# The low halves of the weights move from the Vector engine to GpSimd, and the gated delta rule starts on its queries and keys

## The chip, the cores and the metric

The kernel runs on 1 core of one Trainium2 chip. The metric is the device time of one execution in microseconds (us). Three runs of the kernel before gave 2921.94, 2924.85 and 2926.3 us; the median is 2924.85 us.

The engines are called by their profile names: PE is TensorE (PEld is its weight load), DVE is VectorE, ACT is ScalarE, POOL is GpSimd, SP is SyncE, which here only issues weight transfers.

## The reference

Everything is float32, for 256 tokens of width 2048. Two layers of the first kind each normalize x, multiply by a matrix with 6,668 columns (`w_in`) and feed three mixers: a sliding-window attention (12 query heads, 4 key heads), a convolution module with 31 taps over 512 channels, and a gated delta rule with 6 heads of 128. Their outputs are gated, joined and multiplied by `w_out`.

```
h = rms_norm(x, norm_w[l]);  p = h @ w_in[l]
oa = sliding_window_sink_attention(qa, ka, va, sinks[l]) * silu(za)
ob = conformer_conv_module(ub, ...) * silu(zb)
oc = rms_norm(gated_deltanet(qkv_c, b_c, a_c, ...)) * silu(zc)
x = x + concat([oa, ob, oc]) @ w_out[l]
# inside gated_deltanet:
qkv = silu(causal_depthwise_conv(qkv_raw, conv_w))   # 4 taps, 2304 channels: q, k, v of 768 each
q = l2_norm(q);  k = l2_norm(k)
# then, in chunks of 64 tokens: decays, (I + lower)^-1, a scan over four chunks
```

Two more layers follow, one with a pooling mixer (trailing means over 2, 4, 8 and 16 tokens, then a matrix per group) and one with a gated linear recurrence (LRU: a 4-tap convolution, two block-diagonal gate matrices, a scan over the tokens). Each has its input and output matrices of width 4096 and a gated per-layer embedding after it ("post").

## The kernel before, in words

**Weights.** All matrices lie in one long array (`wall`) in the order in which they are used, cut into chunks, most of them 128 partitions x 2048 floats (1 MB). `sync` (L367) loads chunk c into `W[c % 3]`. For most matrices (`SPLIT`, 388 chunks) the product is made of three passes in the float32r type: ACT copies the chunk into `WH` (the high part, `high`, L857), DVE computes `WL = W - WH` (the low part, `low`, L1340), the activations are split likewise into `HH`/`HL`, `YH`/`YL` or `DH`/`DL`, and PE adds low x high, high x low and high x high (L412). `W`, `WH` and `WL` have three buffers each. The load of chunk c waits for the low part of chunk c-3; the high part of chunk c waits until PE is done with the third chunk before it. The gate matrices of the LRU and two small matrices are used unsplit from `W`; the load behind such a chunk waits for PE itself.

**One program for each engine.** The five functions `tensor`, `vector`, `scalar`, `sync` and `gpsimd` are written out in order, and an engine issues strictly in its order. `tensor`, `vector` and `scalar` walk through the same list of chunks. PE works on a `Group` of chunks (four for 512 columns), whose results lie in a pair of PSUM banks; ACT or DVE take them out behind `group(n)`, which waits for the last chunk. In `tick()` ACT first issues the high part of the chunk two ahead, and DVE the low part of the chunk two ahead, then both call `pump()` four times; PE calls `pump()` four times in a chunk too.

**Side work.** `pump()` moves each active generator one `yield` on. The generators are the delta rule (`decays`, `delta_net`), the convolution (`conformer`, DVE only for its 124 taps), the 4-tap filter of the delta rule (`taps`), `attention`, and in the LRU `conv` and `chain`. The same generator exists for several engines and its `yield` and `rest(n)` counts are set by hand so that the same step comes at the same pump on each. `finish(g)` runs the rest of a generator at once. A generator's step that waits holds up all that the engine's program has behind it, the next high or low part included.

**Around the change.** In `block1` the six groups behind the first eight chunks are the group with 268 columns and the four that give the delta rule its inputs (i = 4, 0, 1, 2, 3 in ACT's and DVE's code; i = 0 to 2 hold queries, keys, 768 channels each, i = 3 and 4 the values). Before, both engines finish the filter and the decays after i = 3 and then begin `delta_net`. In the LRU, `chain(n)` is begun after gate chunk n and has three steps with one `yield` between them, so that all three fall into one tick. `gpsimd` issues only transfers: x to memory and back around each block (its place is scratch meanwhile), a small input and two gain rows for each post stage.

Of the kernel before, what the change touches and what calls it, by code (L numbers as in the profile page):

```python
# [5 lines left out]
F32 = mybir.dt.float32  # L6
# [198 lines left out]
def rest(n):  # L205

    for _ in range(n):
        yield
# [25 lines left out]
def program(nc, wall, tab, pos_d, pT_d, xin, gpost_d, gplo_d, xsave, out):  # L234
# [6 lines left out]
    with ctx:  # L241
# [135 lines left out]
        def gpsimd(e, w):  # L377
            xs_d = xsave.rearrange("(t p) c -> p t c", t=2)
            for l in range(2):
                if l == 0:  # L380
                    for g in range(4):
                        w.wait_ge(*to(f"x{g}", 0))
                else:
                    w.wait_ge(*to("ev_v", 19))
                e.dma_start(xs_d, X[:, :, :]).then_inc(*up("saved", l, by=16))
                w.wait_ge(*to("saved", l))
                w.wait_ge(*to("at_p", l, "turn", 8))
                e.dma_start(X[:, :, :], xs_d).then_inc(*up("back", l, by=16))

            def load_pt(l):  # L390
                e.dma_start(Q[:, 21760:22272], pT_d[:, 512 * l:512 * l + 512]).then_inc(*up("pT", l, by=16))

            def pre_post(l):
                e.dma_start(GP, gpost_d[l:l + 1, :].to_broadcast([128, 2048])).then_inc(*up("gpost", l, by=16))
                e.dma_start(GL, gplo_d[l:l + 1, :].to_broadcast([128, 2048])).then_inc(*up("gple", l, by=16))

            w.wait_ge(*to("norm_v", 2, "hl", 15))
            load_pt(0)
            w.wait_ge(*to("y_v", "pool", 3, 1))
            pre_post(0)  # L400
            w.wait_ge(*to("chunk", ple_end))
            load_pt(1)
            w.wait_ge(*to("y_v", "lru", 7, 1))
            pre_post(1)

        def tensor(e, w):
# [110 lines left out]
            def delta_net(l):  # L517
                yield from rest(3)
# [30 lines left out]
                yield  # L549
                for src, which in ((CV, "tv"), (CK, "tk")):  # L550
                    for k in range(3):
                        b = side(("dn", l, which, k), ("dn_v", l, which, k))
                        for j in range(4):
                            us = slice(128 * (4 * k + j), 128 * (4 * k + j) + 128)
                            i = e.transpose(b[:, 128 * j:128 * j + 128], src[:, us], ident)
                        i.then_inc(*up("dn_p", l, which, k))
                    yield from rest(2)
# [88 lines left out]
            def attention(l):  # L646
# [4 lines left out]
                yield from rest(12)  # L651
# [31 lines left out]
                yield from rest(3)  # L683
                scores(1)
                yield from rest(4)
# [3 lines left out]
                yield from rest(4)  # L689
                turned(1)  # L690
                yield from rest(4)
                turned(2)
                yield from rest(2)
# [17 lines left out]
            def block1(l):  # L711
                proj(l, 512)
                proj(l, 512)
                cf = begin(conformer(l))
                proj(l, 256, "cm+")
                dc = begin(decays(l), first=True)
                for _ in range(4):
                    proj(l, 512)
                finish(dc)
                dn = begin(delta_net(l), first=True)  # L720
                proj(l, 512)
                proj(l, 256)
# [111 lines left out]
        def scalar(e, w):  # L834
# [87 lines left out]
            def delta_net(l):  # L922
                act(sc(0, 3072), sc(4662, 3072), ACT.Square, "dn_a", l, "sq")
# [52 lines left out]
            def attention(l):  # L976
# [8 lines left out]
                yield from rest(12)  # L985
# [24 lines left out]
                yield from rest(3)  # L1010
                scores(1)
                yield from rest(4)
# [3 lines left out]
                yield from rest(4)  # L1016
                turned(1)
                yield from rest(4)
                turned(2)
                yield from rest(2)  # L1020
                yield

            def block1(l):
                w.wait_ge(*to("norm_v", l, "hl", 15))
# [80 lines left out]

            def pool_layer():
# [21 lines left out]
                mix_end = {}  # L1128
                load_u(0)
                for g in range(4):  # L1130
                    for i in range(2):
                        gi = group(4)
                        if g:
                            w.wait_ge(*to("y_v", "pool", g - 1, 1))
                        for b in range(2):
                            act(ZT[:, 4 * i + 2 * b:4 * i + 2 * b + 2, :], pair(bank(gi, b)), ACT.Silu,
                                *(("ev_a", gi) if b else ()))
                    if g > 0:
                        out_part(0, g - 1)
                        oend = here["c"] - 1  # L1140
                    finish(here["win"])
                    for i in range(2):
                        gi = group(2)
                        w.wait_ge(*to("ev_v", gi))
                        if g:
                            w.wait_ge(*to("chunk", oend))
                        act(YH[:, 4 * i:4 * i + 4, :], ZT[:, 4 * i:4 * i + 4, :], ACT.Copy, "y_a", "pool", g, i)
                    mix_end[g] = here["c"] - 1
                    if g < 3:
                        load_u(g + 1)  # L1150
                out_part(0, 3)

            def lru_layer():
# [13 lines left out]
                def chain(n, gi):  # L1167
# [9 lines left out]
                    yield  # L1177
# [3 lines left out]
                    yield  # L1181
# [46 lines left out]
                finish(ch)  # L1228
                out_part(1, 3, halves=2)

            def post(l, n):
                rstd(3 + 4 * l, SM[:, 12:14])
                for i in range(4):
# [9 lines left out]
                    for t in range(2):  # L1243
                        act(E[:, t, 512 * i:512 * i + 512], bank(gi, t), ACT.Copy, *(("ev_a", gi) if t else ()))
                for i in range(4):
                    sumsq(4 + 4 * l, i, JUNK, X, ("x_v", "mid", l, i))
# [41 lines left out]
        def vector(e, w):  # L1288
# [45 lines left out]
            def low(c):  # L1334

                if c >= NCH or c not in split_no:
                    return
                s, m = split_no[c], chunks[c][3] * chunks[c][5]
                w.wait_ge(*to("hi", c))
                e.tensor_tensor(WL[:, s % NSPL, 0:m], W[:, c % NRAW, 0:m], WH[:, s % NSPL, 0:m].bitcast(F32),  # L1340
                                ALU.subtract).then_inc(*up("lo", c))
# [111 lines left out]
            def delta_net(l, zc):  # L1453
                yield from rest(3)
# [108 lines left out]
            def attention(l):  # L1563
# [27 lines left out]
                yield from rest(4)  # L1591
# [36 lines left out]
                yield from rest(3)  # L1628
                scores(1)
                weights(0)  # L1630
                yield from rest(4)
                scores(2)
                weights(1)
                yield from rest(2)
                turned(0)
                weights(2)
                yield from rest(4)
                turned(1)
                yield from rest(4)
                turned(2)  # L1640
                yield from rest(2)
# [7 lines left out]
            def block1(l):  # L1649
# [8 lines left out]
                w.wait_ge(*to("saved", l))  # L1658
                zero(RAW[:, :, 0:3])
                for i in (4, 0, 1, 2, 3):  # L1660
# [7 lines left out]
                    tp = begin(taps(l, i, 4 if i < 4 else 2, g))  # L1668
                finish(tp)
                finish(dc)  # L1670
                dn = begin(delta_net(l, g + 2), first=True)
# [111 lines left out]
            def lru_layer():  # L1783
# [19 lines left out]
                def chain(n, gi, zg):  # L1803
# [12 lines left out]
                    yield  # L1816
# [4 lines left out]
                    yield  # L1821
# [76 lines left out]
            low(0)  # L1898
            low(1)
# [82 lines left out]
```

## Time and profile before

| | |
|---|---|
| runs, us | 2921.94, 2924.85, 2926.3 |
| profiled execution, its own time | 2930.08 us |
| its span | 2928.3 us |
| granted TensorE clock, mean | 0.938 of full |
| PE busy | 2615.5 us (89%) |
| DVE busy | 1683.6 us (57%) |
| ACT busy | 1220.8 us (42%) |
| POOL busy | 6.4 us |
| DMA | 430.61 MB, 147 GB/s |

The profile shows one execution. A row of the views gives a line of the kernel, an engine, an operation, the tensors (out<-in) with their shapes, and how often. Engines overlap, so that busy times don't add to the span; what matters is when PE is idle and who ended its wait. Many rows carry L1305, L1309, L1314 or L843: those are the helpers `tt`, `stt`, `ts` of DVE and `act` of ACT, so that one goes by the tensors there. `Q` is the big scratch, `SM` small columns, `TB` the table of constants, `PS` is PSUM.

### The profile page before, as it was taken

How to read it: one execution, taken by the hardware profiler on the slowest of the kernel's cores; microseconds unless marked ns; L12 is line 12 of the kernel's file. 1: busy time of each engine (PE TensorE's matmuls, PEld its weight loads, DVE VectorE, ACT ScalarE, POOL GpSimd, SP SyncE). 2: the span in 40 equal slices, each digit the busy share in tenths (PEclk: the TensorE clock that was granted, in tenths of full speed). 3: DMA queues.
4: the chain of work that ended last, by engine and by line, in shares of the span. 5: the costliest groups of instructions: out<-in, count | busy, mean ns of one | idle time of the engine just before them, and what ended most of it. 6: DMA issues, size and time to landing. Idle time of an engine off the chain costs nothing.

```text
span 2928.3 us, 39683 instructions
## 1 busy us (share of the span) xinstructions
PE 2615.5 (89%) x17372; PEld 2405.0 (82%) x17372; DVE 1683.6 (57%) x1866; ACT 1220.8 (42%) x1273; POOL 6.4 (0%) x14
## 2 busy tenths in 40 slices
PE   7987998699969996999999999989888988879788
PEld 7986978579969876789989999867888877778666
DVE  4687745555868545555645556655655456445654
ACT  4433234443432244344444334354544444444453
POOL 0000000000000000000000000000000000000000
PEclk9998989899989998999999999999899998989899
DMA  6441222354422212545455545535333434334433
GB/s 223 146 159 73 102 72 103 115 215 146 144 104 98 87 64 109 180 160 184 171 202 187 187 173 188 221 128 200 116 139 145 176 130 172 145 138 164 158 129 129
DMA packets 62493, 430.61 MB, mean 147 GB/s; under 512 B 6896, under 2 KB 7024, under 8 KB 12272
## 3 DMA queue, kind: packets, MB, share of 16 engines
q1 hardware_dynamic: 60496, 414.97, 38.8%
q0 software_dynamic: 1824, 13.11, 1.1%
q8 instruction: 136, 2.23, 0.3%
q14 instruction: 37, 0.30, 0.0%
HBM read 421.76 MB, written 6.29 MB: 146 GB/s over the span
## 4 chain that ended last, share of the span: by engine, by line
PE 69%; DVE 17%; ACT 8%; issue 4%; DMA 2%; DVEq 0%; SPq 0%; ACTq 0%
PE PS L412 68%; DVE WL L1340 4%; ACT Q L843 4%; DVE Q L1309 3%; ACT WH L857 3%; DVE Q L1305 3%; DVE Y L1309 2%; DMA W<-in_wall 2%; DVE Q L1829 1%; DVE X L1309 1%; DVE Q L1314 1%; ACT L843 0%; DVE SM L1324 0%; DVE Q L1316 0%; PE PS L660 0%
## 5 line engine op out<-in xcount | busy, mean ns | idle before, releaser
L1340 DVE TENSOR_TENSOR WL<-W,WH 128x2048 fp32r<-128x2048 f32 (+2 forms) x388 | 860.7, 2225 | 858.8 <-ACT WH L857 858.7
L857 ACT ACTIVATE WH<-W 128x2048 fp32r<-128x2048 f32 (+2 forms) x388 | 717.9, 1858 | 738.9 <-PE PS L412 706.1
L412 PE MATMUL PS<-HH,WL 128*128 128x256 f32 x3392 | 577.4, 291 | 110.7 <-DVE WL L1340 110.0
L412 PEld LDWEIGHTS PS<-HH,WL 128*128 128x128 f32 x3392 | 484.9, 197 | 119.6 <-DVE WL L1340 113.4
L412 PE MATMUL PS<-HL,WH 128*128 128x256 f32 x3392 | 566.7, 288 | 0.0
L412 PE MATMUL PS<-HH,WH 128*128 128x256 f32 x3392 | 564.3, 287 | 0.0
L412 PEld LDWEIGHTS PS<-HL,WH 128*128 128x128 f32 x3392 | 483.2, 197 | 0.0
L412 PEld LDWEIGHTS PS<-HH,WH 128*128 128x128 f32 x3392 | 480.7, 196 | 0.0
L412 PE MATMUL PS<-WL,HH 128*128 128x512 f32 (+2 forms) x768 | 232.3, 384 | 21.8 <-DVE HL L1305 21.8
L412 PE MATMUL PS<-WH,HL 128*128 128x512 f32 (+2 forms) x768 | 225.3, 374 | 0.0
L412 PE MATMUL PS<-WH,HH 128*128 128x512 f32 (+2 forms) x768 | 223.8, 372 | 0.0
L843 ACT ACTIVATE Q<-PS 128x512 f32<-128x512 f32 (+1 forms) x136 | 80.5, 592 | 297.5 <-PE PS L412 268.6
L412 PE MATMUL PS<-Q 128*128 128x128 f32 (+5 forms) x1320 | 180.3, 293 | 15.7 <-DVE Q L1305 11.9
L412 PEld LDWEIGHTS PS<-Q 128*128 128x128 f32 (+2 forms) x1320 | 162.9, 193 | 33.3 <-DVE Q L1305 12.7
L412 PEld LDWEIGHTS PS<-WL,HH 128*128 128x128 f32 x768 | 141.7, 194 | 49.6 <-issue 24.0
L412 PE MATMUL PS<-WL,YH 128*128 128x512 f32 x512 | 158.9, 392 | 10.4 <-DVE O L1305 10.4
L412 PEld LDWEIGHTS PS<-WH,HL 128*128 128x128 f32 x768 | 144.3, 194 | 27.4
L412 PEld LDWEIGHTS PS<-WH,HH 128*128 128x128 f32 x768 | 143.5, 193 | 26.8
L412 PE MATMUL PS<-WH,YL 128*128 128x512 f32 x512 | 158.6, 391 | 0.0
L412 PE MATMUL PS<-WH,YH 128*128 128x512 f32 x512 | 158.6, 391 | 0.0
L843 ACT ACTIVATE Q<-Q 128x1024 f32<-128x1024 f32 (+4 forms) x62 | 66.1, 1066 | 136.6 <-DVE Q L1309 97.8
L412 PEld LDWEIGHTS PS<-WL,YH 128*128 128x128 f32 x512 | 96.3, 189 | 30.7 <-issue 11.2
(126 smaller groups left out, 2086.2 us busy)
## 6 DMA issues: line engine op xcount, KB each, us to landing
W<-in_wall SPq DMA_DIRECT2D x378, 1024.0 KB, 4.8
W<-in_wall SPq DMA_DIRECT2D x16, 512.0 KB, 3.4
W<-in_wall SPq DMA_DIRECT2D x8, 536.0 KB, 3.3
xsave<-X POOLq DMA_DIRECT2D x2, 2048.0 KB, 11.9
X<-xsave POOLq DMA_DIRECT2D x2, 2048.0 KB, 11.4
X<-in_x SPq DMA_DIRECT2D x4, 512.0 KB, 7.4
Q<-in_g_post POOLq DMA_DIRECT2D x2, 1024.0 KB, 4.9
Q<-in_g_ple_out POOLq DMA_DIRECT2D x2, 1024.0 KB, 7.4
```

Source lines behind the costliest of these rows:

```text
L412: return e.matmul(o, l, r, start=start, stop=stop, skip_group_check=True)
L843: e.activation(o, a, f, **k).then_inc(*up(*sig))
L857: e.activation(WH[:, s % NSPL, 0:m], W[:, c % NRAW, 0:m], ACT.Copy).then_inc(*up("hi", c))
L1305: e.tensor_tensor(o, a, b, op).then_inc(*after(sig))
L1309: e.scalar_tensor_tensor(out=o, in0=a, scalar=s, in1=b, op0=op0, op1=op1).then_inc(*after(sig))
L1314: e.tensor_scalar(o, a, s1, None, op0).then_inc(*after(sig))
L1340: e.tensor_tensor(WL[:, s % NSPL, 0:m], W[:, c % NRAW, 0:m], WH[:, s % NSPL, 0:m].bitcast(F32), ALU.subtract).then_inc(*up("lo", c))
L1829: e.tensor_tensor_scan(TA[:, js], R[:, js], IG[:, js], 0.0, ALU.mult, ALU.add).then_inc(*after(()))
```

## The change

GpSimd gets a program of its own with one instruction for each split chunk, `WL = W - WH`, which waits only for that chunk's high part; DVE's `low` is gone. The transfers that GpSimd issued are now issued by ACT, at places in its order. The delta rule's generator is begun one group earlier (behind i = 2) with 16 more rests, and the filter of the values (i = 3) isn't finished at once but runs beside it; PE waits for its result (`cs 3`) before it turns the values. Rests of `attention` are longer, and `chain` of the LRU has three rests where one `yield` was.

```diff
         def gpsimd(e, w):
-            xs_d = xsave.rearrange("(t p) c -> p t c", t=2)
...
-            w.wait_ge(*to("y_v", "lru", 7, 1))
-            pre_post(1)
+            for c in split_at:
+                s, m = split_no[c], chunks[c][3] * chunks[c][5]
+                w.wait_ge(*to("hi", c))
+                e.tensor_tensor(WL[:, s % NSPL, 0:m], W[:, c % NRAW, 0:m], WH[:, s % NSPL, 0:m].bitcast(F32),
+                                ALU.subtract).then_inc(*up("lo", c))
@@ tensor
             def delta_net(l):
-                yield from rest(3)
+                yield from rest(16 + 3)
...
                 yield
+                w.wait_ge(*to("dn_a", l, "cs", 3))
                 for src, which in ((CV, "tv"), (CK, "tk")):
...
@@ tensor, attention
-                yield from rest(12)
+                yield from rest(10)
...
                 scores(0)
-                yield from rest(3)
+                yield from rest(6)
                 scores(1)
-                yield from rest(4)
+                yield from rest(6)
                 scores(2)
                 yield from rest(2)
                 turned(0)
-                yield from rest(4)
+                yield from rest(6)
                 turned(1)
-                yield from rest(4)
+                yield from rest(5)
                 turned(2)
-                yield from rest(2)
+                yield from rest(3)
@@ tensor, block1
-                for _ in range(4):
+                for _ in range(3):
                     proj(l, 512)
                 finish(dc)
                 dn = begin(delta_net(l), first=True)
+                proj(l, 512)
                 proj(l, 512)
@@ scalar
             def delta_net(l):
+                yield from rest(16)
                 act(sc(0, 3072), sc(4662, 3072), ACT.Square, "dn_a", l, "sq")
...
                 turned(2)
-                yield from rest(2)
+                yield from rest(3)
+                w.wait_ge(*to("at_p", l, "turn", 8))
+                e.dma_start(X[:, :, :], xs_d).then_inc(*up("back", l, by=16))
...
             def block1(l):
+                if l:
+                    w.wait_ge(*to("ev_v", 19))
+                else:
+                    for g in range(4):
+                        w.wait_ge(*to(f"x{g}", 0))
+                e.dma_start(xs_d, X[:, :, :]).then_inc(*up("saved", l, by=16))
...
-                    tp = begin(taps(l, i, 4 if i < 4 else 2))
-                finish(tp)
-                finish(dc)
-                dn = begin(delta_net(l), first=True)
+                    begin(taps(l, i, 4 if i < 4 else 2))
+                    if i == 2:
+                        finish(dc)
+                        dn = begin(delta_net(l), first=True)
...
@@ scalar, lru chain (the same two lines change in vector)
                         act(SQ2[:, c_], R[:, c_], ACT.Square, "step_a", "sq", n, k)
-                    yield
+                    yield from rest(3)
...
                         act(TA[:, c_], TA[:, c_], ACT.Sqrt, "step_a", "rt", n, k)
-                    yield
+                    yield from rest(3)
@@ vector
-            def low(c):
...
             def tick(again=False):
                 if not again:
-                    low(here["c"] + NSPL - 1)
                     here["c"] += 1
...
             def taps(l, i, n, g):
+                w.wait_ge(*to("saved", l))
                 w.wait_ge(*to("ev_a", g))
...
             def delta_net(l, zc):
-                yield from rest(3)
+                yield from rest(16 + 3)
```

Vector's `block1` and the scalar and vector copies of `attention` change like those of the other engines; in vector's `attention` `weights(0)` and `weights(1)` now come ahead of the next `scores`, and `weights(2)` behind `turned(0)` and its rests. ACT's issues of the small input and of the gain rows stand behind a wait of their own, in `pool_layer`, `lru_layer` and `post`.

## Rows read from the trace of the kernel before

**Rows 1.** The page, part 1 (busy us) and part 5 (a group: busy, mean ns | idle before).

```profile
PE 2615.5 (89%) x17372; PEld 2405.0 (82%) x17372; DVE 1683.6 (57%) x1866; ACT 1220.8 (42%) x1273; POOL 6.4 (0%) x14
...
L843 ACT ACTIVATE Q<-PS 128x512 f32<-128x512 f32 (+1 forms) x136 | 80.5, 592 | 297.5 <-PE PS L412 268.6
```

**Rows 2.** Waits of PE, whole span: what waited <- releaser, total us, times, longest.

```profile
PE PS L412 <- DVE WL L1340: 110.0, 15, 14.7
PE PS L412 <- DVE SM L1314: 68.1, 6, 16.1
PE PS L412 <- ACT Q L843: 35.7, 3, 18.1
```

**Rows 3.** Stretches (A:B length, busy of PE, PEld, DVE, ACT, POOL; clock, DMA share, GB/s).

```profile
100.00:225.00 125.00, 108.16 (x861) 107.55 (x860) 101.44 (x178) 47.30 (x44) 0.00 (x0) 0.92 0.40 143
137.00:143.00 6.00, 5.73 (x27) 5.74 (x28) 5.71 (x10) 2.60 (x2) 0.00 (x0) 0.52 0.68 212
1300.00:1900.00 600.00, 598.75 (x4396) 572.41 (x4396) 341.87 (x250) 240.40 (x167) 1.06 (x2) 1.00 0.51 187
```

**Rows 4.** Groups of DVE instructions by shape, 1300 to 1900 us: count | busy, mean ns | idle before.

```profile
L1340 DVE TENSOR_TENSOR WL<-W,WH 128x2048 fp32r<-128x2048 f32 x106 | 242.0, 2291 | 204.5 <-ACT WH L857 204.5
L1305 DVE TENSOR_TENSOR Q<-Q 128x1024 f32<-128x1024 f32 x28 | 34.2, 1223 | 0.7
```

**Rows 5.** Waits of PE in the LRU, 2160 to 2740 us.

```profile
PE PS L412 <- DVE WL L1340: 88.2, 7, 14.7
```

**Rows 6.** ACT in order of time, 2215 to 2246 us (start, duration).

```profile
2222.22 1.92 ACT L857 ACTIVATE WH<-W 128x2048 fp32r<-128x2048 f32 x1 [2.81 <-DMA W<-in_wall]
2236.33 1.06 ACT L843 ACTIVATE Q<-Q 128x1024 f32<-128x1024 f32 x1 [0.66 <-DVE Q L1314]
2242.83 1.06 ACT L843 ACTIVATE YH<-Q 128x1024 fp32r<-128x1024 f32 x1 [5.45 <-DVE Q L1305]
2243.80 5.49 ACT L857 ACTIVATE WH<-W 128x2048 fp32r<-128x2048 f32 x3
```

**Rows 7.** DVE and PE in the same stretch.

```profile
2224.17 2.29 DVE L1340 TENSOR_TENSOR WL<-W,WH 128x2048 fp32r<-128x2048 f32 x1 [2.41 <-ACT WH L857]
2245.72 6.70 DVE L1340 TENSOR_TENSOR WL<-W,WH 128x2048 fp32r<-128x2048 f32 x3 [0.58 <-ACT WH L857]
2248.07 1.22 PE L412 MATMUL PS<-HH,WL 128*128 128x256 f32 x4 [13.15 <-DVE WL L1340]
```

**Rows 8.** The start of the delta rule, 195 to 235 us: DVE, ACT, PE.

```profile
220.95 6.21 DVE L1309 SCALAR_TENSOR_TENSOR Q<-Q,TB 128x256 f32<-128x256 f32 x12
216.92 1.06 ACT L843 ACTIVATE Q<-Q 128x1024 f32<-128x1024 f32 x1 [10.97 <-DVE Q L1309]
229.96 2.75 ACT L843 ACTIVATE Q<-Q 128x3072 f32<-128x3072 f32 x1
232.76 8.19 PE L412 MATMUL PS<-Q,TB 128*128 128x512 f32 x12 [17.31 <-ACT Q L843]
```

**Rows 9.** Waits of PE in the attention of layer 0, 478 to 550 us.

```profile
PE PS L679 <- DVE Q L1309: 10.8, 1, 10.8
PE PS L412 <- DVE HL L1305: 10.8, 1, 10.8
```

**Rows 10.** Groups of DVE instructions by shape, 100 to 225 us.

```profile
L1340 DVE TENSOR_TENSOR WL<-W,WH 128x2048 fp32r<-128x2048 f32 x17 | 38.9, 2287 | 16.5 <-ACT WH L857 16.5
L1309 DVE SCALAR_TENSOR_TENSOR Y<-Q,TB,Y 128x256 f32<-128x256 f32 x57 | 27.5, 483 | 1.5
L1309 DVE SCALAR_TENSOR_TENSOR Q<-Q,TB 128x256 f32<-128x256 f32 x50 | 24.3, 486 | 1.7
L1314 DVE TENSOR_SCALAR Q<-Q,TB 128x256 f32<-128x256 f32 x18 | 6.4, 355 | 3.4 <-ACT Q L843 2.5
```

**Rows 11.** DMA issues (size, median us to landing), and POOL's issue (count | busy, mean ns).

```profile
W<-in_wall SPq DMA_DIRECT2D x378, 1024.0 KB, 4.8
L385 POOL DMA_DIRECT2D xsave<-X x2 | 1.6, 778 | 99.5 <-DVE X L1305 88.0 <-DMA X<-in_x 11.5
```

More of the change, by code:

```diff
@@ L377, in gpsimd @@
         def gpsimd(e, w):
-            xs_d = xsave.rearrange("(t p) c -> p t c", t=2)
[L379 to L402, printed above, removed]
-            w.wait_ge(*to("y_v", "lru", 7, 1))
-            pre_post(1)
+            for c in split_at:
[3 more added lines that the diff above has]
+                                ALU.subtract).then_inc(*up("lo", c))
         def tensor(e, w):
@@ L984, in attention @@
                 act(sm[:, 0:32], sm[:, 0:32], ACT.Exp, "at_a", l, "rs", scale=-0.5, bias=0.0)
-                yield from rest(12)
+                yield from rest(10)
                 for k in range(5):
@@ L1009, in attention @@
                 scores(0)
-                yield from rest(3)
+                yield from rest(6)
                 scores(1)
-                yield from rest(4)
+                yield from rest(6)
                 scores(2)
@@ L1015, in attention @@
                 turned(0)
-                yield from rest(4)
+                yield from rest(6)
                 turned(1)
-                yield from rest(4)
+                yield from rest(5)
                 turned(2)
-                yield from rest(2)
+                yield from rest(3)
+                w.wait_ge(*to("at_p", l, "turn", 8))
+                e.dma_start(X[:, :, :], xs_d).then_inc(*up("back", l, by=16))
                 yield
+            xs_d = xsave.rearrange("(t p) c -> p t c", t=2)
             def block1(l):
+                if l:
[4 more added lines that the diff above has]
+                e.dma_start(xs_d, X[:, :, :]).then_inc(*up("saved", l, by=16))
                 w.wait_ge(*to("norm_v", l, "hl", 15))
@@ L1104, in out_part, with load_pt, load_gains @@
                             sumsq(3 + 4 * l, i, JUNK, O, ("ev_v", gi))
+            def load_pt(l):
+                e.dma_start(Q[:, 21760:22272], pT_d[:, 512 * l:512 * l + 512]).then_inc(*up("pT", l, by=16))
+            def load_gains(l):
+                e.dma_start(GP, gpost_d[l:l + 1, :].to_broadcast([128, 2048])).then_inc(*up("gpost", l, by=16))
+                e.dma_start(GL, gplo_d[l:l + 1, :].to_broadcast([128, 2048])).then_inc(*up("gple", l, by=16))
             def pool_layer():
@@ L1128, in pool_layer @@
                 mix_end = {}
+                w.wait_ge(*to("norm_v", 2, "hl", 15))
+                load_pt(0)
                 load_u(0)
@@ L1150, in pool_layer @@
                         load_u(g + 1)
+                w.wait_ge(*to("y_v", "pool", 3, 1))
+                load_gains(0)
                 out_part(0, 3)
@@ L1228, in lru_layer @@
                 finish(ch)
+                w.wait_ge(*to("y_v", "lru", 7, 1))
+                load_gains(1)
                 out_part(1, 3, halves=2)
@@ L1244, in post @@
                         act(E[:, t, 512 * i:512 * i + 512], bank(gi, t), ACT.Copy, *(("ev_a", gi) if t else ()))
+                if l == 0:
+                    load_pt(1)
                 for i in range(4):
@@ L1332, in zero @@
                 e.memset(o, 0.0).then_inc(*after(sig))
-            def low(c):
[L1336 to L1341, printed above, removed]
             def tick(again=False):
                 if not again:
-                    low(here["c"] + NSPL - 1)
                     here["c"] += 1
@@ L1453, in delta_net @@
             def delta_net(l, zc):
-                yield from rest(3)
+                yield from rest(16 + 3)
                 rn = sc(0, 3072)
@@ L1590, in attention @@
                          *(("at_v", l, "kr") if t else ()))
-                yield from rest(4)
+                yield from rest(2)
                 yield from rest(3)
@@ L1627, in attention @@
                 scores(0)
-                yield from rest(3)
+                yield from rest(6)
+                weights(0)
                 scores(1)
-                weights(0)
-                yield from rest(4)
+                yield from rest(6)
+                weights(1)
                 scores(2)
-                weights(1)
                 yield from rest(2)
                 turned(0)
+                yield from rest(6)
                 weights(2)
-                yield from rest(4)
                 turned(1)
-                yield from rest(4)
+                yield from rest(5)
                 turned(2)
-                yield from rest(2)
+                yield from rest(3)
                 for n in range(3):
@@ L1657, in block1 @@
                 cf = begin(conformer(l))
-                w.wait_ge(*to("saved", l))
                 zero(RAW[:, :, 0:3])
@@ L1667, in block1 @@
                         dc = begin(decays(l), first=True)
[L1668 to L1671, printed above, removed]
+                    begin(taps(l, i, 4 if i < 4 else 2, g))
+                    if i == 2:
+                        finish(dc)
+                        dn = begin(delta_net(l, g + 3), first=True)
                 group(4)
@@ L1815, in chain @@
                     tt(IG, IG, UC, ALU.mult)
-                    yield
+                    yield from rest(3)
                     for k, c_ in enumerate(cut):
@@ L1820, in chain @@
                         ts(TA[:, c_], TA[:, c_], 0.0, None, ALU.max, None, "step_v", "ta", n, k)
-                    yield
+                    yield from rest(3)
                     j0 = 4 * (n % 2)
@@ L1897, in vector @@
             norm("norm_w", 0, 0, 0)
-            low(0)
-            low(1)
             rope_tables()
```

## The prediction

> **What bounds the kernel now.** I read the page first: PE is busy 89% of the span, no other engine is near (DVE 57%, ACT 42%) [rows 1]. So only PE's idle time, some 310 us, and its slow clock can be won back. The waits of PE say who ended that idle time: 110.0 us in 15 waits were ended by DVE's low part (`WL`), 68.1 by the norms' columns (`SM`), 35.7 by ACT in `Q` [rows 2]. The norms' part isn't touched by the change: it is a serial chain of squares, sum and rstd. The stretches tell where PE is at its limit: from 1300 to 1900 us (pooling) it is busy 598.75 of 600 us at full clock [rows 3], so nothing is to be won there, and since 106 split chunks pass in it [rows 4] a chunk takes 600/106 = 5.66 us. That is the pace that a low part on any engine must keep.
>
> Of the 110 us, 88.2 lie in seven waits in the LRU [rows 5]. The order of time shows why: ACT's high part of one chunk starts at 2222.22, the next three only at 2243.80, because `chain` runs all its steps in one tick and ACT waits in it for DVE; then comes DVE's low, and PE goes on at 2248.07 after 13.15 us of idleness [rows 6, 7]. The 35.7 us of ACT are mostly two waits at the start of the delta rule, one per layer: DVE filters the values (12 instructions from 220.95), only then ACT squares queries and keys (229.96), and PE had been idle for 17.31 us [rows 8].
>
> **The subtraction on GpSimd.** POOL executes no arithmetic in this trace, so its price must be bounded. The same shape takes 2.29 us on DVE [rows 4] and 1.92 us for a copy on ACT [rows 6]. Lower end: 2.29. Upper end: an engine that fetches its two operands one after the other, so that it pays two passes of DVE's length, 4.6 us. I take the upper end, because DVE's row is that of an engine that takes both operands at once, and nothing shows that POOL does. 388 of them are then at most 388 x 4.6 = 1785 us in a span of 2928: it fits, and in the pooling layer it is 106 x 4.6 = 488 of 600 us. The Trainium skill ("GPSIMD Engine Reference", 3.1 Elementwise) gives 4497 ns for a float32 `tensor_tensor` of 2048 elements; no row here shows it, and the sum would be the same by it.
>
> Latency: the high part of a chunk starts when PE is done with the third chunk before it, so PE has two chunks, 11.3 us, before it needs the low part. Before: 1.9 + 2.3 = 4.2 us, or 5.4 behind an eviction of 2 x 0.59 us [rows 1]. After: 6.5 or 7.7. Slack is still 3.6 us. The ring of `W`: a load starts at the low part and lands 4.8 us later [rows 11], so 6.5 + 4.8 + 0.5 = 11.8 us, or 13.0, before 3 x 5.66 = 17.0. Both hold. Only where ACT is late already is the added 2.3 us seen on PE: at the very first chunk, and in the rest of each LRU stall. I charge 3 us outside the LRU (bounds 0 and 10).
>
> **LRU, -46 us.** Two effects. DVE no longer stands in `low` (2224.17, after 2.41 us of waiting for ACT, 2.29 long [rows 7]): what comes behind it, the first step of the chain included, is 4.7 us earlier, and so is ACT's square root, from 2236.33 to 2231.6; it ends at 2232.7. With three rests instead of one `yield` only two steps fall into the tick, so ACT makes the next high part there, 2232.7 to 2234.6, instead of at 2243.80 behind `YH` [rows 6]. POOL has the low part at 2239.2. PE became idle at 2248.07 - 13.15 = 2234.9, so it waits 4.4 us; the high part behind `YH` costs another 1.6. So 6 us of each stall stay, 7 x 6 = 42 of 88.2, and 46 go. Bounds: 0 (ACT as late as before) and 88. The clock gives nothing back: a wait of 3.4 us before 137 us was followed by a granted clock of 0.52, the level of 1.2 GHz, in the next 6 us [rows 3], so a short stall costs what a long one does.
>
> **Low waits in the blocks, -18 us.** 110.0 - 88.2 = 21.8 us are left, 5.5 of them the first chunk (it is charged above). The other waits, 3 to 4 us each, come where DVE is in its filter backlog when the high part is ready; POOL isn't. Some 15 us go, and about half of the slow clock behind four of them, 6 us at half speed losing 3 us each: another 5, less 2 for contention. Bounds 0 and 27.
>
> **Start of the delta rule, -26 us.** The square now needs only i = 0 to 2. Its last filter was ready at 216.92 [rows 8], and that was after 10.97 us in which ACT waited for a DVE that had four `low` of 2.29 us in that group. Even at 216.92, eviction (1.2), one high part (1.9) and the square (2.75) end at 224, 8.7 us before 232.76; with the 9.2 us of `low` gone it ends near 215, when PE asks for it. I take 13 of 17.3 us in each layer: 26. Bounds 10 and 35. The values' filter now lies over the next four chunks; the wait for `cs 3` comes 17 pumps behind the group and the filter ends at pump 16: one pump to spare, about 1.4 us, so this wait is late next. Behind it in PE's order stand the matmuls of the current chunk.
>
> **Attention, -25 us.** PE waits 10.8 + 10.8 us and small ones in one layer [rows 9], like it in the other, 53 in all. They follow a chain DVE, ACT, DVE through three groups of heads, in which DVE also waits for high parts that ACT makes behind its exponentials. The rests between the steps grow from 19 to 28, 9 pumps or 2.25 chunks, 12.7 us a layer of other matmuls over the same chain. I take half of 53, less 2. Bounds 0 and 50. The cost if rests are too long is `finish`, but 52 pumps stand against 41 rests.
>
> **Transfers on ACT, 0.** Eight issues of about 0.8 us [rows 11] in a kernel where ACT is busy 42%. The wait for `turn 8` stands three pumps behind that step on PE and should be over; behind it ACT has the next high part. The reload has two output groups to land. Bounds 0 and +6.
>
> **Contention, +25 us and +5.** In 100 to 225 us DVE is busy 101.44 of 125 us [rows 3]: 38.9 in 17 `low`, and 27.5 + 24.3 + 6.4 = 58.2 in filter instructions on SBUF alone [rows 10]. Without `low`, DVE has 62.5 left and all could lie beside POOL: no cost, even a gain. If POOL and these instructions exclude each other, POOL's 17 x 4.6 = 78 and the 58.2, with small ones 62, make 140 in place of 125: +15, and more where DVE's order passes it on. Nothing in the trace shows POOL computing beside DVE, so I take +12.5 for each layer's filter stretch. In the pooling layer exclusion would make 488 + 34.2 (28 additions) + some 40 of other SBUF instructions = 562 of 600 [rows 4]: it fits on average and not always: +5. Bounds for all: -10 and +75.
>
> **Sum.** 3 - 46 - 18 - 26 - 25 + 0 + 25 + 5 = -82 us against the profiled execution's own 2930.08: 2848. The median of the runs is 5 us under that execution: 2843 us.
>
> **Rivals.**
> (a) Full exclusion. POOL's subtraction and each DVE instruction with two SBUF operands run only one after the other. For it: both filter stretches would be over-full as worked out. Against: the pooling layer has room. Price: +20 for each filter stretch, +10 for each delta rule behind it, +15 pooling, and 15 of the LRU's gain, since the chain's scans come to stand behind low parts: 90 in place of the 30 charged, so 2843 + 60 = 2903. The Trainium skill ("SBUF — State Buffer", Who interferes with whom) speaks for this: a DVE instruction with two SBUF inputs and a GpSimd instruction that reads SBUF hold one shared port in turn, each for its whole length. No run here shows it yet.
> (b) Slower: the subtraction itself is the pace. If it takes three DVE passes (6.9 us) it exceeds 5.66, and PE waits in every stretch where it is now busy. It binds in the pooling layer (106 chunks), and in the LRU and the posts, where PE is at its pace between its stalls (I estimate 125 more), about 230 chunks x 1.3 us = +300, and gives 2843 + 300, about 3145. The change turns to a loss from about 5.66 + 82/230 = 6.0 us. Against: this is 2.6 times DVE's row.
> (c) All is hidden: no contention and a low part of about 2.3 us. Then LRU -75, low waits -27, delta rule -35, attention -45, contention -10: -192, less 5: 2733.
> (d) The change doesn't do what it says: PE's waits only get another name (ACT's order ends them, not DVE's), and contention eats the rest: 2925.
>
> **Chances.** Forecast 0.50, (a) 0.19, (b) 0.12, (c) 0.12, (d) 0.07. What this kernel's measurement can tell from no change is about 0.2%, 6 us. Faster: 0.50 + 0.19 + 0.12 less 0.04 for exclusion that costs more than worked out = 0.77; same 0.05; slower 0.18. The range reaches towards (c) and past (a) and leaves out most of (b): 2750 to 2945 us.
>
> **What would show it.** POOL with 388 subtractions of 4.6 us mean; DVE's busy time near 820 us, 1683.6 less 388 low parts of 2.2. PE's waits on `WL`, now POOL's, near 50 us in the LRU and none in the blocks. PE's wait for ACT at the delta rule under 5 us. DVE's filter rows at 0.48 us mean if there is no exclusion; longer rows, or gaps between them, if there is. The pooling stretch still at 5.66 us a chunk. The prediction is wrong if POOL's row is over 5.6 us, or if PE in the pooling layer waits for POOL.

## The result

The kernel after takes 3005.39 us (median of 4 runs, 3005.12 to 3006.71) against 2924.11 before: ratio 1.0279, 95% interval 1.0261 to 1.0297. I had forecast 2843 us, and the time lies outside the range as well. The profiled execution has a span of 3003.5 us, 75.2 more than before. Of these, 59.0 us are more idle time of PE, and 16.2 are longer busy time for the same 17372 matmuls (2615.5 to 2631.7 us; the mean granted clock fell from 0.938 to 0.933 of full).

PE's first matmul of each norm marks the layers in both traces (16.1, 651.0, 1276.7, 1950.0, 2062.3 and 2817.0 us before; 16.8, 674.3, 1329.6, 2024.3, 2138.4 and 2892.7 after), and the differences tell where the time went: block 0 +22.6, block 1 +29.6, pooling layer +21.4, first post +1.8, LRU -0.4, last post -0.5, start +0.7: 75.2.

The page after, busy times (part 1) and groups (part 5: shapes, count | busy, mean ns | idle before), beside [rows 1]:

```profile
PE 2631.7 (88%) x17372; PEld 2414.4 (80%) x17372; DVE 1386.4 (46%) x1478; ACT 1219.6 (41%) x1273; POOL 1747.9 (58%) x392
...
L381 POOL TENSOR_TENSOR WL<-W,WH 128x2048 fp32r<-128x2048 f32 (+2 forms) x388 | 1747.7, 4517 | 1234.3 <-ACT WH L837 1233.5
```

The subtraction on GpSimd takes 4.5 us in the mean over all sizes (median 4.615), as assumed. The Trainium skill's 4497 ns for 2048 elements ("GPSIMD Engine Reference", 3.1 Elementwise) agrees with this trace, where that size takes 4492 ns at the least and 4617 in the median. But DVE lost 861 us of subtractions and is busy only 297 us less (1386 us, where I had forecast near 820): its other instructions became 564 us longer. The groups by shape say which:

```profile
L1315 DVE SCALAR_TENSOR_TENSOR Y<-Q,TB,Y 128x256 f32<-128x256 f32 x240 | 236.5, 985 | 9.4
L1315 DVE SCALAR_TENSOR_TENSOR Q<-Q,TB 128x256 f32<-128x256 f32 x204 | 218.2, 1069 | 7.3
L1320 DVE TENSOR_SCALAR Q<-Q,TB 128x256 f32<-128x256 f32 x68 | 124.3, 1828 | 163.0 <-ACT Q L823 160.8
...
L1315 DVE SCALAR_TENSOR_TENSOR HL<-PS,TB,HH 128x256 fp32r<-128x256 f32 x96 | 46.5, 484 | 30.1 <-ACT HH L823 25.2
L1311 DVE TENSOR_TENSOR Q<-Q,PS 128x512 f32<-128x512 f32 x60 | 41.3, 688 | 20.6 <-PE PS L390 18.6 <-DVE Q L1311 0.5
```

The filters (`SCALAR_TENSOR_TENSOR`, which here read two operands in SBUF) went from 483 and 486 ns [rows 10] to 985 and 1069, the tensor_scalar from 355 to 1828, but instructions that take one operand from PSUM (`HL<-PS`, `Q<-Q,PS`) have the 484 and 688 ns of before. In order of time (start, duration), DVE and then GpSimd (its view ends at 180 us; the second series has three subtractions):

```profile
142.39 4.73 DVE L1315 SCALAR_TENSOR_TENSOR Y<-Q,TB,Y 128x256 f32<-128x256 f32 x1
147.16 4.61 DVE L1320 TENSOR_SCALAR Q<-Q,TB 128x256 f32<-128x256 f32 x1
151.80 4.72 DVE L1315 SCALAR_TENSOR_TENSOR Y<-Q,TB,Y 128x256 f32<-128x256 f32 x1
156.56 0.35 DVE L1320 TENSOR_SCALAR Q<-Q,TB 128x256 f32<-128x256 f32 x1
156.95 0.49 DVE L1315 SCALAR_TENSOR_TENSOR Y<-Q,TB,Y 128x256 f32<-128x256 f32 x1
```

```profile
137.51 18.73 POOL L381 TENSOR_TENSOR WL<-W,WH 128x2048 fp32r<-128x2048 f32 x4
172.66 9.09 POOL L381 TENSOR_TENSOR WL<-W,WH 128x2048 fp32r<-128x2048 f32 x2 [16.42 <-ACT WH L837]
```

While GpSimd makes four subtractions back to back, DVE gets one small instruction in for each, so an instruction of 0.35 or 0.48 us takes 4.6 to 4.7; when GpSimd pauses at 156.2 us the next ones have their old length. That is rival (a)'s mechanism, turns on the SBUF operands. The Trainium skill states such an exclusion for a DVE instruction with two SBUF inputs beside a GpSimd instruction that reads SBUF ("SBUF — State Buffer", Who interferes with whom); this trace agrees for DVE, with 4.73 us in place of 0.48. GpSimd loses little by it: 18.73 us for four are 4.68 each, 0.07 over the median, so DVE's 0.35 to 0.48 us are not added in full. Then the delay feeds itself, as ACT shows:

```profile
168.41 1.06 ACT L823 ACTIVATE Q<-Q 128x1024 f32<-128x1024 f32 x1 [15.68 <-DVE Q L1315]
169.56 1.23 ACT L823 ACTIVATE Q<-PS 128x512 f32<-128x512 f32 x2
170.68 5.50 ACT L837 ACTIVATE WH<-W 128x2048 fp32r<-128x2048 f32 x3
```

ACT waits 15.68 us for the late filter, then hands GpSimd three high parts at once, and the next series of back-to-back subtractions slows DVE again. PE's waits and stretches after, beside [rows 2, 3, 5] (the waits in the LRU, 2230 to 2850 us, come last):

```profile
PE PS L390 <- POOL WL L381: 133.9, 36, 13.2
PE PS L390 <- DVE HL L1311: 39.1, 6, 17.7
PE PS L390 <- ACT Q L823: 25.1, 2, 12.8
...
100.00:225.00 125.00, 101.96 (x793) 100.94 (x793) 113.01 (x125) 44.13 (x40) 73.43 (x17) 0.90 0.38 135
1350.00:1950.00 600.00, 585.58 (x4292) 561.60 (x4291) 168.27 (x135) 230.11 (x158) 471.19 (x102) 0.99 0.50 179
...
PE PS L390 <- POOL WL L381: 68.0, 17, 13.2
PE PS L390 <- DVE O L1311: 21.1, 2, 10.5
```

In the filter stretch PE falls from 108.2 to 102.0 us busy. The pooling layer, where PE hardly waited, makes 102 chunks in 600 us instead of 106. PE's waits on GpSimd's low part from norm to norm of that layer (1329.7 to 2024.3 us):

```profile
PE PS L390 <- POOL WL L381: 15.5, 8, 3.3
```

The prediction named this as a sign of being wrong. In the LRU's gate part, which [rows 5] cover, the waits on the low part fall from 88.2 to 54.8 us. The other 13.2 of the 68.0 stand in its output stage, outside [rows 5], where PE had waited 10.4 us for DVE. Two waits of 10.5 us on DVE's output additions are new. The layer as a whole gains only 0.4 us.

The start of the delta rule after, PE, beside [rows 8]:

```profile
242.92 7.38 PE L390 MATMUL PS<-Q,TB 128*128 128x512 f32 x12 [12.29 <-ACT Q L823]
279.11 1.19 PE L390 MATMUL PS<-Q 128*128 128x128 f32 x4 [13.19 <-DVE Q L1311]
```

The first wait fell from 17.31 to 12.29 us, where I had forecast under 5, and the next hand-over from DVE, which had cost 1.3 us, costs 13.19.

### The profile page after: what moved, and what is told of

The parts are those of the page before. It is cut to its first block, busy times and chain, and to the rows that moved or that the text cites. A ratio compares the mean times of both kernels' runs of the same rounds, so it can differ in the third digit from the quotient of the medians.

```text
span 3003.5 us, 39655 instructions
## 1 busy us (share of the span) xinstructions
PE 2631.7 (88%) x17372; PEld 2414.4 (80%) x17372; DVE 1386.4 (46%) x1478; ACT 1219.6 (41%) x1273; POOL 1747.9 (58%) x392
## 4 chain that ended last, share of the span: by engine, by line
PE 61%; DVE 25%; ACT 7%; POOL 3%; issue 3%; DMA 1%; DVEq 0%; ACTq 0%; SPq 0%
PE PS L390 60%; DVE Q L1315 6%; DVE Q L1311 5%; ACT Q L823 5%; DVE Y L1315 4%; DVE Q L1320 3%; POOL WL L381 3%; DVE Q L1825 1%; ACT WH L837 1%; DVE QA L1311 1%; DVE HL L1311 1%; DVE SM L1330 1%; DVE SM L1320 1%; DMA W<-in_wall 0%; DVE SM L1315 0%
## 5 line engine op out<-in xcount | busy, mean ns | idle before, releaser
L381 POOL TENSOR_TENSOR WL<-W,WH 128x2048 fp32r<-128x2048 f32 (+2 forms) x388 | 1747.7, 4517 | 1234.3 <-ACT WH L837 1233.5
L1315 DVE SCALAR_TENSOR_TENSOR Y<-Q,TB,Y 128x256 f32<-128x256 f32 x240 | 236.5, 985 | 9.4
L1315 DVE SCALAR_TENSOR_TENSOR Q<-Q,TB 128x256 f32<-128x256 f32 x206 | 221.8, 1077 | 30.4 <-ACT Q L823 23.1
L1320 DVE TENSOR_SCALAR Q<-Q,TB 128x256 f32<-128x256 f32 x68 | 124.3, 1828 | 163.0 <-ACT Q L823 160.8
L1311 DVE TENSOR_TENSOR Q<-Q 128x1024 f32<-128x1024 f32 (+2 forms) x58 | 108.3, 1868 | 146.2 <-ACT Q L823 144.3
```

The lines of the kernel that those rows point to most:

```text
L1311: e.tensor_tensor(o, a, b, op).then_inc(*after(sig))
L1315: e.scalar_tensor_tensor(out=o, in0=a, scalar=s, in1=b, op0=op0, op1=op1).then_inc(*after(sig))
L1320: e.tensor_scalar(o, a, s1, None, op0).then_inc(*after(sig))
```

## The experiments

"E1" and so on are the kernels; all times are medians, all intervals 95%, against the kernel before in the same call (2924 to 2928 us).

**E1, the subtraction back on DVE, the rest of the change kept.** In part:

```diff
 # gpsimd: empty; vector:
 def tick(again=False):
     if not again:
+        low(here["c"] + NSPL - 1)
         here["c"] += 1
```

> The kernel after with the subtraction back on the Vector engine, two chunks ahead in its tick, and GpSimd idle; all else of the change stays. Theory A (GpSimd's subtraction costs all, by shutting out Vector instructions on SBUF operands and by 2.3 us more latency; the other parts help): the filter rows return to 0.48 us, time 2840 to 2890 us, ratio to before 0.97 to 0.99. Theory B (the other parts cost time too, or give nothing): 2915 to 2960 us.

2911.06 us, ratio 0.9952 (0.9937 to 0.9967). The filter rows are at 484 and 485 ns. Moving the subtraction costs 3005 - 2911 = 94 us; the other parts are worth 14, not the 40 to 80 of theory A. The time lies between the two ranges, 4 us under theory B's.

**E2, the kernel before with the subtraction on GpSimd and the transfers on ACT, nothing else.**

> The kernel before with only the subtraction on GpSimd and the transfers on the Scalar engine; rests, chain and delta rule as before. Theory A: slower than the kernel after, 3050 to 3100 us, because the other parts of the change had won 40 to 80 us. Theory B: about 3005 us, as the kernel after.

3021.86 us, 1.0333 (1.0317 to 1.0348). The subtraction alone costs 97 us, and the other parts give 16 beside it. It fits E1; the time lies between the two theories: A's sign is right and its size is not.

**E3 and E5, GpSimd writes the tile and reads nothing.** The edits, shortened:

```diff
-e.tensor_tensor(WL[...], W[...], WH[...].bitcast(F32), ALU.subtract).then_inc(*up("lo", c))
+e.memset(WL[:, s % NSPL, 0:m].bitcast(F32), 0.0).then_inc(*up("lo", c))       # E3
+for k in (m, m, 3 * m // 8): memset of k columns, each behind the last one    # E5
```

> The kernel after with one GpSimd memset of the same tile in place of the subtraction; it leaves out the low parts, which are zero. GpSimd then reads no SBUF and takes about 2 us. If shutting out or latency is the cause, Vector's filter rows fall from 1.0 to 0.48 us mean and the time to 2780 to 2860 us. If something else in the change costs the time, it stays near 3000 us.

> The kernel after with three GpSimd memsets of the low part's tile, one behind the other (2048, 2048 and 768 columns, some 4.6 us together), in place of the subtraction; it leaves out the low parts. GpSimd then is as late as in the kernel after but reads no SBUF. Theory A1 (the shutting out of Vector costs, the latency little): 2740 to 2800 us, near the 2722 of the single memset. Theory A2 (the latency of 4.6 us costs): 2880 to 3000 us.

E3: 2721.53 us, 0.9303 (0.9287 to 0.9318), 58 us below the expected range. A memset takes 1.811 us (median). E5: 2767.28 us, 0.9463 (0.9448 to 0.9477); GpSimd is busy 1644.5 us, 4.24 for each chunk, against 1.76 in E3 and 4.50 in the kernel after. DVE's groups in E3 (two) and E5 (one):

```profile
L1314 DVE SCALAR_TENSOR_TENSOR Y<-Q,TB,Y 128x256 f32<-128x256 f32 x240 | 116.4, 485 | 40.3 <-PE PS L389 31.6
L1319 DVE TENSOR_SCALAR Q<-Q,TB 128x256 f32<-128x256 f32 x68 | 41.5, 611 | 162.8 <-ACT Q L822 160.6
L1323 DVE TENSOR_SCALAR Q<-Q,TB 128x256 f32<-128x256 f32 x68 | 67.9, 999 | 161.0 <-ACT Q L826 158.8
```

The filter rows are at 485 ns in both; the SBUF tensor_scalar is not back at 355. So the longer GpSimd work costs 2767 - 2722 = 46 us, for a later low part and for these longer tensor_scalars together (DVE is busy 904.9 us against 868.7; not separated). The reading by GpSimd costs 3005 - 2767 = 238. Against E1, a DVE without subtractions would be worth 2911 - 2722 = 190 us if GpSimd's help were free: -190 + 46 + 238 is the +94 of E1. Some 5 us of the 238 are latency too, 0.26 us more at E5's price; on the other side E5 still holds the tensor_scalars, so not all exclusion is in the 238.

Could PE be faster only because the low parts are zero? No: in the pooling layer, at full clock in both, a matmul on the low part (`HH,WL`) takes 283 ns in the median in E3 as in E1.

**E4, each subtraction in four parts.**

```diff
+q = m // 4
+for j in range(4):
+    v = slice(q * j, q * j + q)
+    i = e.tensor_tensor(WL[:, s % NSPL, v], W[:, c % NRAW, v], WH[:, s % NSPL, v].bitcast(F32), ALU.subtract)
+i.then_inc(*up("lo", c))
```

> The kernel after with each GpSimd subtraction cut into four instructions of a quarter of the columns. If Vector gets in one instruction for each GpSimd instruction (turns), it now waits 1.2 us for a turn instead of 4.6, four times as many get in, and the time falls to 2900 to 2950 us. If only the sum of both engines' times counts, it stays at 3005 us or grows by GpSimd's issue cost (3 x 388 x 0.1 us at most).

2958.37 us, 1.0112 (1.0097 to 1.0127): 47 us faster than the kernel after, though GpSimd does the same work, and 8 us above the range for turns. DVE's order of time in E4, and GpSimd's 20 quarters back to back beside it:

```profile
150.95 1.40 DVE L1319 SCALAR_TENSOR_TENSOR Y<-Q,TB,Y 128x256 f32<-128x256 f32 x1
152.38 1.40 DVE L1319 SCALAR_TENSOR_TENSOR Q<-Q,TB 128x256 f32<-128x256 f32 x1
153.82 1.40 DVE L1319 SCALAR_TENSOR_TENSOR Y<-Q,TB,Y 128x256 f32<-128x256 f32 x1
```

```profile
131.18 28.05 POOL L384 TENSOR_TENSOR WL<-W,WH 128x512 fp32r<-128x512 f32 x20 [2.72 <-ACT WH L841]
```

One DVE instruction for each GpSimd instruction, now each 1.4 us: turns. The cut has a price: GpSimd is busy 1983.8 us against 1747.9, 0.2 us for each of the 1164 added instructions, not the 0.1 expected. The pooling layer takes 704.2 us (694.7 after, 673.3 before). Four quarters take 5.4 us there in the median, and in 40 of 108 chunks they take more than the pace of 5.66.

**E13, E14 and E16, the filter stretch alone.** Base is E9 (below, 2901.8 us); GpSimd serves the 16 chunks of each block beside which DVE filters: whole, in four parts, or with a memset.

```diff
+def on_pool(c):          # in part
+    return any(za_end[l] - 42 <= c < za_end[l] - 26 for l in range(2))
```

> The kernel before with the rests of the LRU's chain and the transfers on the Scalar engine (2901.8 us), and the subtraction whole on GpSimd for the 16 chunks of each block beside which Vector filters (32 chunks of 388), on Vector elsewhere. If this stretch carries the loss in the blocks, each block takes some 15 to 30 us more: 2932 to 2962 us. If the loss is spread over the whole block, 2902 to 2915 us.

> The same 32 subtractions in four parts each. Turns: Vector gets one SBUF instruction in for each quarter (1.4 us), so the stretch loses less than half of the whole ones' loss. Sum of both engines' times: the same loss, since 16 x 4.6 us and Vector's 58 us have to fit in the same time.

> The same 32 chunks with one GpSimd memset of the low part's tile in place of the subtraction; it leaves out these low parts. GpSimd reads nothing and Vector is free of 32 subtractions. If the reading is the cause, no filter row is longer than 0.49 us and each block is 10 to 20 us shorter: 2862 to 2882 us.

E13: 2940.50 us, 1.0044 (1.0029 to 1.0059), which is 35 us over E9 by the two ratios, 1.1 us for each of 32 subtractions; block 0 takes 652.2 us from norm to norm against 631.3 in E9. E14: 2924.56 us, 0.9989 (0.9980 to 0.9999), 19 us over E9. E16: 2871.06 us, 0.9811 (0.9796 to 0.9825), 33 us faster than E9; its filters are at 485 ns, but its SBUF tensor_scalars in this stretch at 651, over the 0.49 us expected of all filter rows. The stretch carries a large part of the blocks' loss: the two blocks together are 37 us longer in E13 than in E9, and 47 in the kernel after than in E1. Four parts save 16 of 35 us, which the intervals don't tell from half. Why they don't save it all was not shown apart. E14's trace has two things that fit: each small DVE instruction still takes 1.4 us in turns, three times its length, and 20 quarters in turns take 28.02 us, 5.6 for a chunk where the whole subtraction takes 4.6. A plain sum of both engines' times is not what is paid: 1.25 us (a quarter at its shortest) and 0.48 would be 1.73 for each turn, and it is 1.43. E13's filter stretch, 100 to 225 us, against [rows 10]:

```profile
L1325 DVE SCALAR_TENSOR_TENSOR Y<-Q,TB,Y 128x256 f32<-128x256 f32 x49 | 40.7, 830 | 1.9
L1330 DVE TENSOR_SCALAR Q<-Q,TB 128x256 f32<-128x256 f32 x14 | 33.9, 2422 | 5.2 <-ACT Q L834 4.7
L1325 DVE SCALAR_TENSOR_TENSOR Q<-Q,TB 128x256 f32<-128x256 f32 x35 | 17.0, 486 | 1.3
```

That is 98 filter instructions instead of 125 in the same time.

**E7, E6 and E9, the other parts.** On E1: E7 has the chain of the LRU with one `yield` again, E6 the attention as before, E9 attention and delta rule as before (so it is the kernel before with the chain's rests, and the transfers on ACT).

```diff
-                    yield from rest(3)      # E7, twice in scalar and in vector
+                    yield
```

> The kernel with the subtraction on Vector (2911 us) and the LRU's chain with one yield between its steps, as before. Its LRU took 734 us against 755 before. If the rests of the chain are all of that, this is slower by 20 us (2931); if the delta rule or the transfers moved something, by less.

> The kernel with the subtraction on Vector (2911 us) and the attention's rests and order as before the change. If the longer rests are worth the 25 us that I forecast, it is slower by some 25 us; if they only move the wait, as the 7.6, 14.8 and 10.9 us waits in the attention of that kernel suggest, it is the same or up to 10 us faster.

> The kernel before with the rests of the LRU's chain and the transfers on the Scalar engine, and nothing else; subtraction on Vector, delta rule and attention as before. If the early start of the delta rule gives nothing (its 9 us earlier first sum is given back at the next hand-overs), the time is that of the kernel with it, 2908 us, within 4. If it was worth the 26 us that I forecast, this is 2934 us.

E7: 2930.53 us, 1.0021 (1.0009 to 1.0032): the rests of the chain are worth 20 us, all that the other parts give and more. E6: 2908.16 us, 0.9949 (0.9933 to 0.9965), not told apart from E1: the attention's rests give nothing. E9: 2901.78 us, 0.9925 (0.9912 to 0.9939): against E6 (0.9949) the early start of the delta rule costs some 6 us, hardly beyond the noise, and is no gain. PE in E1 shows why:

```profile
224.16 7.16 PE L386 MATMUL PS<-Q,TB 128*128 128x512 f32 x12 [9.10 <-ACT Q L819]
251.75 5.36 PE L386 MATMUL PS<-Q 128*128 128x128 f32 x32 [4.82 <-DVE Q L1307]
...
276.82 1.54 PE L530 MATMUL PS<-TB,Q 128*128 128x128 f32 x6 [2.95 <-ACT Q L819]
```

The wait of 17.31 us [rows 8] is 9.10 and PE is there 8.6 us earlier, but PE waits 4.82 us at the next hand-over from DVE (1.3 before), and the 2.95 for the values are new.

**E8, E11 and E10, GpSimd in the LRU alone.** E8 is E1 with four parts there, E11 with whole ones, E10 is E9 with four parts.

```diff
+def on_pool(c):
+    return lru0 <= c <= lru1
```

> The subtraction on Vector everywhere but in the LRU layer, where GpSimd makes it in four parts. By the stretches of the runs so far (LRU 721.6 us with four parts on GpSimd, 734.3 on Vector) 2898 us. If the gain there hangs on the layers before, 2911.

> The subtraction on GpSimd in the LRU layer alone as there, but whole, not in four parts (delta rule and attention as in the kernel after). If Vector gets one turn for each GpSimd instruction, its SBUF instructions in the LRU wait up to 4.6 us and the LRU takes the 754 us of the kernel after, so 2895 + 32 = 2927 us. If the gain is that Vector's order is free, it stays at 2895 us.

> The same with the subtraction on GpSimd in four parts in the LRU layer alone. If the parts add, 2908 less the 15.7 us that this gave beside the other parts: 2892 us, ahead of all kernels so far that compute everything.

E8: 2895.39 us, 0.9901 (0.9880 to 0.9923). E11: 2938.53 us, 1.0048 (1.0035 to 1.0062), 11 us over its forecast. The cut alone is worth 43 us here (the LRU takes 722.0 us with quarters, 761.2 with whole ones, 734.3 with DVE's subtraction in E1), so the loss in the LRU is the length of a turn: DVE's chain of small instructions that ACT and PE wait for. E10: 2895.13 us, 0.9900 (0.9887 to 0.9914), ahead of E9 by 7 us, not 16: the gains don't add, and why was not shown.

**E12 and E15, towards the best of both.** E12 is E10 with four parts also in the attention and output stretches of the blocks; E15 adds the stretch beside the delta rule.

> The subtraction on GpSimd in four parts in the LRU layer and in both attention and output stretches of the blocks, on Vector elsewhere. Vector has few instructions on two SBUF operands there, and waits in its order for high parts. If freeing its order is worth what the attention's waits (some 30 us a layer) suggest, 2870 to 2885 us; if those waits are a chain of Vector and Scalar that stands anyway, 2895 us or a little more for the latency.

> The fastest kernel so far (2866.7 us; four parts on GpSimd in the LRU and in the attention and output stretches) with GpSimd also for the chunks beside the delta rule, so that Vector subtracts only beside the filter, the pooling layer and the posts. Vector's part there is mostly on PSUM operands, which GpSimd leaves alone; if so it is 2855 to 2867 us. If the 124 taps of the convolution, which run there too, take their turns in front of the delta rule's steps, 2867 to 2900 us.

E12: 2866.65 us, 0.9801 (0.9788 to 0.9814), the fastest that computes everything, 58 us ahead of before and 139 ahead of after, and 3 us below the expected range. It is 28 us ahead of E10. PE's waits in the attention of block 0 (470 to 545 us) are 17.7 us against 25.3 in E10, which is about half of the 14 us that the block gained. E15: 2880.81 us, 0.9836 (0.9820 to 0.9853), 10 us slower than E12 by the ratios: the expectation's second case; that it is the taps which take turns in front of the delta rule's steps was not shown apart.

## Why the prediction was wrong

**What failed: "Contention, +25 us and +5".** It priced exclusion, where it priced it at all, as a sum of busy times (140 in place of 125 us), took about half, and charged nothing outside the filter stretches and the pooling layer. The reading costs 238 us (E5 against the kernel after), of which I had charged 30. By the traces of these two kernels (240 us) the two blocks have 145 of it, the pooling layer 24 and the LRU 69, where I had charged 25, 5 and 0. Two things were missing. Turns: DVE gets one instruction for each GpSimd instruction however short it is, so a stretch of small instructions stands nearly still while GpSimd has work (E4, E11 against E8). And the return: a late DVE holds ACT, ACT delivers high parts in a burst, GpSimd runs back to back, where the sum counted on an even spread; the traces show this loop, and no run took it alone. The granted clock fell with it: 45 of the 240 us are PE's own busy time (2586.5 us at a mean granted clock of 0.964, 2631.7 at 0.933), for which the contention had no term.

**Rival (a)** had the mechanism and the sign of the correction, and with 90 us for it the same fault of size: it gave 2903. It too left the kernel faster than before. Rival (b) fell: 4.5 us is not over the pace, yet the loss threshold was reached without it.

**The subtraction at 4.6 us** was right in size; the reason given for it (two operands fetched one after the other) was a guess that no run here tests. **Its latency** was sized at 3 us outside the LRU; E5 against E3 gives 46 us in all for 2.5 us more (LRU 684.9 against 660.1, the two blocks together 1167.9 against 1150.4), the longer tensor_scalars included. The slack of 3.6 us was worked out for a regular run of chunks; that it is missing behind evictions with side work is my reading, not shown wait by wait.

**LRU, -46.** The rests of the chain are worth 20 us (E7) with DVE's subtraction. The part that should come from freeing DVE's order came with quarters, 16 us (E8), and as a loss of 27 with whole ones (E11). Together 36 of the 46, in a kernel that isn't this one.

**Low waits in the blocks, -18.** They grew: six of 4.1 to 10.6 us in the two filter stretches, where four of 3.3 to 4.0 had been.

**Delta rule, -26.** Even with DVE's subtraction the first wait fell by 8.2 us in a layer, not 13 (E1), and what came next was late; net +6 (E9 against E6). I had named the values' wait as next and priced it at nothing. The larger one is the hand-over before it: in E1 DVE runs 13 filter instructions of the values and two subtractions in front of it (238.47 to 249.23 us), which I had not counted. In the kernel after three of these filters take 4.6 to 4.7 us each in turns, and PE waits 13.19 us there.

**Attention, -25.** The rests gave 0 (E6). Taking the subtraction out of DVE's order in the attention and output stretches gave 28 us (E12 against E10).

**The transfers on ACT, 0,** are not separated: they are in E1 and E9 alike, and E9 with them is 22 us faster than before.

The size of the whole: 2843 us forecast, 3005 measured. Of the 162 us between, 208 are contention (238 less 30) and 43 latency (46 less 3); against them stands that a DVE free of the subtraction (190 us) and the other parts (14) are worth 89 more than the 115 that I had for them together. That this sum closes proves nothing: its terms are differences between the same runs. The forecast's gain of 115 was too low and its costs were too low by more.

## What to carry to other kernels

Before work on two SBUF operands goes to GpSimd, count DVE's instructions on SBUF operands beside it, not their time: each may wait out one GpSimd instruction. Give GpSimd such work only where DVE mostly reads PSUM or is idle, and cut it (here from 4.6 to 1.3 us) as long as the pieces keep the pace. Other cuts than four were not tried, and beside the delta rule the cut work still cost 10 us (E15). A moved wait is worth what stays behind it: try each part alone, since here one of four carried the gain and the largest step the loss.

## What the runs showed of the hardware

A GpSimd subtraction of 128x2048 float32 took 4.617 us (median), a quarter of it 1.296 (E4), so a cut into four costs some 0.6 us. A GpSimd memset of the tile took 1.811 us; beside it DVE's filters on two SBUF operands kept their 485 ns, but a `TENSOR_SCALAR` from SBUF to SBUF rose from 355 to 611 ns (E3), and to 999 beside three memsets (E5): that form is held by a writing GpSimd as well. DVE instructions with a PSUM operand kept their length beside everything (of 96 `HL<-PS` none took over 487 ns in the kernel after). Turns cost GpSimd less than the length of DVE's instruction: four whole subtractions in turns took 18.73 us, 4.68 each, and 20 quarters in turns 28.05 us, 1.40 each, where a quarter took 1.25 at the least.
